# A hybrid decoder trunk with a grouped mixture of experts: ScalarE issues the up matrices' reloads

## The chip, the cores and the metric

The kernel runs on one core of a Trainium2 chip. The metric is the device time of one launch in microseconds (us); the median of several launches is given. The engines of the core are TensorE (PE in the profile; its weight loads are PEld), VectorE (DVE), ScalarE (ACT), GpSimd (POOL) and SyncE (SP). SP does nothing but issue transfers (DMAs); ACT and POOL can issue transfers too. All transfers are carried by the core's 16 DMA engines.

## The reference, cut to what matters

```python
def moe_ffn(x, router_w, router_b, w1, w3, w2):
    e_idx, gates = route(xf, router_w, router_b)      # top group, then 2 of its 8 experts
    ...
    def one_block(args):
        toks, e = args
        xb = x_pad[toks]
        hb = jax.nn.silu(xb @ w1[e]) * (xb @ w3[e])
        return hb @ w2[e]
    ...
def reference(x, ...):
    for l in range(DEPTH):                            # DEPTH = 2
        mix = hybrid_mixer(x, ...)
        x = layer_norm(ALPHA * x + mix, ln1_g[l], ln1_b[l])
        ffn = moe_ffn(x, router_w, router_b, w1[l], w3[l], w2[l])
        x = layer_norm(ALPHA * x + ffn, ln2_g[l], ln2_b[l])
    return x
```

There are 256 tokens of width 1024, two layers, and 64 experts in each. Each expert has a gate matrix `w1` and an up matrix `w3` (1024 x 256) and a down matrix `w2` (256 x 1024), all float32, so each of the three is 1 MB (1.0486 million bytes).

## The kernel before

Both layers do the same: a token mixer (projections, three kinds of attention, an output projection), then routing, then the experts. The experts of a layer are worked through in 16 batches of 4 (`NB = 4`). A batch needs 12 matrices, 12 MB, and every matrix of all 64 experts is read, since the order of the work doesn't depend on which experts are chosen. The texts below number the batches of a layer 0 to 15, and the four experts of a batch k = 0 to 3.

**Buffers.** There are two sets of slots, `w_even` and `w_odd` in the profile: batch j uses the set of its parity. In a set each k has a slot for gate and up matrix side by side (`w13_slots[parity][k]`, gate first) and one for the down matrix (`w2_slots[parity][k]`). Both sets for batches 0 and 1 are loaded (but for one down matrix) before the experts begin. A slot is loaded for batch j + 2 once batch j is through with it.

**TensorE, one batch (`batch`, line 1081).** For k = 0 to 3 it multiplies the gathered tokens by gate and up matrix at once (`up_gate`, line 1030, L1040 in the profile; it waits for `w13_in[parity][k]`, which counts both transfers, and raises `part_psum`). Then it folds the partial sums (L1053) as soon as VectorE has copied those of k = 0 and 2 and ScalarE those of k = 1 and 3. It turns the gates (L1059), gathers the tokens of the next batch (L1025), turns the hidden rows (L1066), multiplies them by the four down matrices (L1072, raises `y2_psum`), and adds the rows to the output (L1078). Then the next batch begins. The last batch of a layer is cut finer: its last gate matrix has a semaphore of its own (`w1_last_in`), and its down matrices come in six pieces (`w2_last_in`, LAST_COLS), filled up with idle multiplications (L609).

**SyncE (`load_first`, line 467; `load_batch`, line 473).** One queue issues everything. For batch j + 2 it waits for `part_psum` of batch j, k; issues gate and up matrix of that k (L380); after the four k it waits for `y2_psum` of batch j and issues the four down matrices (L384). Then it goes on to the next batch, and behind the last batch to the next layer's first weights.

**ScalarE, one batch (line 1828).** It copies the partial sums of k = 1 and of k = 3 (`copy_partial`, L1657), takes a tanh (`squash`, L1822), and makes three more copies: the turned gates, half of the gathered tokens, half of the output rows. Each waits for TensorE. In the first batch of a layer it also seeds the output banks with x (`seed`) between the copies of k = 1 and 3. In the kernel before ScalarE issues one transfer in all, at the very start.

Of the kernel before, what the change touches and what calls it, by code (L numbers as in the profile page):

```python
# [29 lines left out]
NE, NG, EPG, FE, TOP_K = 64, 8, 8, 256, 2  # L30
BLK = 32
NB = P // BLK
BATCHES = NE // NB
# [47 lines left out]
def program(nc, a, consts, const_at, out):  # L81
# [10 lines left out]
    w1 = a["moe_w1"].rearrange("l e (p c) f -> (l e) p (c f)", c=DC)  # L92
    w3 = a["moe_w3"].rearrange("l e (p c) f -> (l e) p (c f)", c=DC)
# [5 lines left out]
    with ctx:  # L99
# [16 lines left out]
        def w13_views(mem):  # L116
            return [mem[:, k * W13:(k + 1) * W13].rearrange("p (m c f) -> p m c f", m=2, c=DC) for k in range(NB)]
# [4 lines left out]
        w13_slots = [w13_views(w13_even), w13_views(w13_mem)]  # L122
# [148 lines left out]
        w13_in = [[Signal(f"w13_{parity}_in{k}") for k in range(NB)] for parity in ("even", "odd")]  # L271
# [55 lines left out]
        def after(eng, l, sig, n):  # L327

            eng.wait_ge(sig.sem, l * sig.per_layer + (n + sig.start))

        def plain(eng):

            eng.sem_inc(passed.sem, 1)
# [5 lines left out]
        def start_batches(eng, base, l):  # L339

            after(eng, l, routed, 1)
            plain(eng)
            m = eng.value_load(iters[0:1, 0:1], min_val=BATCHES - 2, max_val=BATCHES * MAX_ROUNDS - 2)
            return m, batches_before(eng, base)
# [13 lines left out]
        def _(sp):  # L358
# [3 lines left out]
            for l in range(DEPTH):  # L362
# [11 lines left out]
                def load_w_out(h):  # L374
                    sp.dma_start(w_out_half[h], w_out[l, :, :, h * 512:(h + 1) * 512]).then_inc(w_out_in[h].sem, 16)

                def load_w13(e, k, parity, last=False):
                    for m, w in enumerate((w1, w3)):
                        sig = w1_last_in if last and m == 0 and k == NB - 1 else w13_in[parity][k]
                        sp.dma_start(w13_slots[parity][k][:, m, :, :].rearrange("p c f -> p (c f)"),  # L380
                                     w[l * NE + e * NB + k]).then_inc(sig.sem, 16)

                def load_w2(e, k, parity):
                    sp.dma_start(w2_slots[parity][k].rearrange("p c d -> p (c d)"),  # L384
# [44 lines left out]

                after(sp, l, comb, 4)  # L430
                load_w13(0, 0, 0)
                load_w13(0, 1, 0)
                after(sp, l, upT_psum, 2)
                load_ln(sp, l, 0)
                after(sp, l, comb, 8)
                load_w13(0, 2, 0)
                load_w13(0, 3, 0)
                load_w_out(0)
# [26 lines left out]
                m, b0 = start_batches(sp, base, l)  # L465

                def load_first(j, back, e, parity, last=False):
                    for k in range(NB):
                        sp.wait_ge(part_psum.sem, (b0 + j) * NB + (part_psum.start + k + 1 - back))
                        plain(sp)  # L470
                        load_w13(e, k, parity, last)

                def load_batch(j, back, e, parity, last=False):
                    load_first(j, back, e, parity, last)
                    sp.wait_ge(y2_psum.sem, (b0 + j) + (y2_psum.start + 1 - back // NB))
                    plain(sp)


                load_first(2, 2 * NB, 2, 0)
                after(sp, l, x0_ready, 2)  # L480
                after(sp, l, x1_ready, 2)
# [8 lines left out]
                with sp.Fori(4, m, 2) as j_even:  # L490
                    for parity in range(2):
                        j = j_even + parity
# [8 lines left out]
                last = l * NE + (BATCHES - 1) * NB  # L501
# [1147 lines left out]
        def _(act):  # L1649
# [6 lines left out]
            def copy(dst, src):  # L1656
                return fn(dst, src, ACT.Copy)  # L1657
# [4 lines left out]
            for l in range(DEPTH):  # L1662
# [126 lines left out]
                def seed(t):  # L1789
                    for h in range(2):  # L1790
                        after(act, l, y_set, 2 * t + h + 1)
                        after(act, l, (x0_ready, x1_ready)[t], h + 1)
                        copy(Y[t][h][:, :], x[:, t, h * 512:(h + 1) * 512]).then_inc(y_seeded.sem, 1)
# [10 lines left out]
                m, b0 = start_batches(act, base, l)  # L1804

                def copy_gathered(g):
                    act.wait_ge(gathered[1].sem, g + 1)
                    copy(xg[:, 4:8, :], bank[3][:, :].rearrange("p (c s) -> p c s", c=4)).then_inc(xg_act.sem, 1)
# [3 lines left out]
                for c in range(2):  # L1812
                    last = fn(xg[:, 4 + c, :], bank[3][:, c * P:(c + 1) * P], ACT.Identity,
                              scale=g_cols[:, 0, 4 + c:5 + c], bias=g_cols[:, 1, 4 + c:5 + c])
                last.then_inc(first_mid_sb.sem, 1)

                def copy_partial(b, k):
                    act.wait_ge(part_psum.sem, b * NB + (part_psum.start + k + 1))
                    copy(partial[:, k, :], bank[k % 2][:, :]).then_inc(part_act.sem, 1)

                def squash():
                    return fn(eg, bank[0][:, 0:FE], ACT.Tanh, scale=0.5).then_inc(eg_ok.sem, 1)  # L1822

                def copy_scatter(b, source):
                    act.wait_ge(scT_psum.sem, b + 1)
                    copy(scatter, source[:, 0:SEQ]).then_inc(scT_sb.sem, 1)

                def batch(j, first=False):
                    b = b0 + j
                    copy_partial(b, 1)  # L1830
                    if first:
                        seed(0)
                        seed(1)
                        after(act, l, y_seeded, 4)
                    copy_partial(b, 3)
                    act.wait_ge(gu_psum.sem, b + 1)
                    squash()
                    copy_scatter(b, bank[1])
                    copy_gathered(b + 1)
                    act.wait_ge(y2_psum.sem, b + (y2_psum.start + 1))  # L1840
                    copy(y_rows[:, 512:1024], bank[3][:, :]).then_inc(y2_act.sem, 1)

                def last_batch(j):
# [12 lines left out]
                    act.wait_ge(y2_psum.sem, b + (y2_psum.start + 1))  # L1856
                    copy(y_rows[:, end:], bank[0][:, 0:DM - end]).then_inc(y2_act.sem, 1)

                batch(0, first=True)
                with act.Fori(1, m) as j:  # L1860
                    batch(j)
                batch(m)
                last_batch(m + 1)
                act.reg_add(base, base, m + 2)
# [20 lines left out]
```

## Time and profile before

| | us |
|---|---|
| median of 3 launches | 1169.85 (1169.73 to 1171.15) |
| the profiled launch | 1170.28 |
| its span, first to last instruction | 1168.3 |
| TensorE busy | 1050.2 (90%) |
| ScalarE busy | 202.5 (17%) |
| VectorE busy | 368.0 (31%) |
| experts of the first layer, TensorE | about 149 to 581 |
| experts of the second layer, TensorE | about 727 to 1158 |

The profile is one launch. Its page gives busy time by engine, then the span in 40 slices of 29.2 us, then groups of instructions and transfers. Some 2.0 us of the profiled launch lie outside the span.

### The profile page before, as it was taken

The page shows a single profiled execution, that of the slowest core. Times are in us where ns is not written, and L with a number is a line of the kernel's source. Part 1 is how long each engine was busy: PE and PEld are TensorE (multiplying, and loading weights), DVE is VectorE, ACT ScalarE, POOL GpSimd, SP SyncE. Part 2 cuts the span into 40 slices and gives each one's busy share as a digit, 9 for nine tenths or more (in the row PEclk, how much of TensorE's full clock was granted, in tenths as well). Part 3 has the DMA queues.
Part 4 walks back from the last instruction along what each step waited for, and adds up shares of the span by engine and source line. Part 5 has one row for each costly group of instructions (what it writes and reads, how often), then busy time and mean ns, then how long its engine had stood idle before and what let it go on. Part 6 is the DMA issues. An engine that isn't in the chain of part 4 may idle for free.

```text
span 1168.3 us, 16442 instructions
## 1 busy us (share of the span) xinstructions
PE 1050.2 (90%) x6190; PEld 590.4 (51%) x6190; DVE 368.0 (31%) x1009; ACT 202.5 (17%) x473; POOL 32.3 (3%) x46
## 2 busy tenths in 40 slices
PE   9999989989988988888999999989988998888885
PEld 6665754445544444444456657445544444444443
DVE  4875541111122111111268657311122111111113
ACT  1244221111111111111121532211111111101011
POOL 0010010000000000000000101000000000000001
PEclk9999999999999999989999999999999999989898
DMA  9957699999999999999995776999999999999997
GB/s 311 334 226 288 271 376 419 420 420 421 421 420 420 422 420 420 421 420 418 385 331 201 280 297 257 412 421 422 418 421 421 420 420 421 420 420 421 421 419 261
DMA packets 94084, 442.70 MB, mean 379 GB/s; under 512 B 18273, under 2 KB 37857, under 8 KB 45921
## 3 DMA queue, kind: packets, MB, share of 16 engines
q1 hardware_dynamic: 93760, 441.60, 94.1%
q0 software_dynamic: 144, 0.58, 0.1%
q8 instruction: 21, 0.34, 0.1%
q14 instruction: 15, 0.11, 0.0%
q10 hardware_dynamic: 144, 0.07, 0.0%
HBM read 441.16 MB, written 1.05 MB: 379 GB/s over the span
## 4 chain that ended last, share of the span: by engine, by line
PE 57%; SPq 29%; DVE 5%; DMA 5%; issue 3%; ACT 1%; POOL 0%; DVEq 0%; POOLq 0%
SPq L380 19%; PE bank L1025 10%; PE bank L1040 10%; SPq L384 10%; PE bank L674 9%; PE bank L1072 6%; PE bank L1078 5%; DMA w_odd<-in_moe_w 5%; PE bank L800 4%; PE bank L664 2%; PE bank L1053 2%; PE bank L934 1%; ACT moe L1657 1%; PE bank L770 1%; DVE moe L1603 1%
## 5 line engine op out<-in xcount | busy, mean ns | idle before, releaser
L1025 PE MATMUL bank<-moe,x 128*128 128x128 f32 x960 | 233.0, 402 | 0.0
L1025 PEld LDWEIGHTS bank<-moe,x 128*128 128x128 f32 x960 | 230.7, 334 | 0.0
L1657 ACT ACTIVATE moe<-bank 128x512 f32<-128x512 f32 (+2 forms) x194 | 102.1, 535 | 728.2 <-PE bank L1040 347.1
L1078 PE MATMUL bank<-moe 128*128 128x512 f32 (+1 forms) x264 | 119.3, 593 | 25.3 <-DVE moe L1603 24.1
L1040 PE MATMUL bank<-w_even,moe 128*32 128x512 f32 x1024 | 115.9, 600 | 14.5 <-DMA w_even<-in_moe_w 13.0
L1040 PE MATMUL bank<-w_odd,moe 128*32 128x512 f32 x992 | 116.6, 616 | 13.2 <-DMA w_odd<-in_moe_w 13.2
L1576 DVE COPY moe<-bank 128x512 f32<-128x512 f32 x64 | 44.3, 692 | 246.0 <-PE bank L1040 245.8
L1078 PEld LDWEIGHTS bank<-moe 128*128 128x128 f32 x264 | 47.2, 189 | 98.6 <-DVE moe L1603 51.3
L674 PE MATMUL bank<-w_even,w_odd 128*128 128x384 f32 x240 | 81.3, 489 | 0.0
L1040 PEld LDWEIGHTS bank<-w_even,moe 128*32 128x32 f32 x1024 | 31.3, 110 | 94.7 <-issue 70.0
L1040 PEld LDWEIGHTS bank<-w_odd,moe 128*32 128x32 f32 x992 | 30.1, 111 | 94.4 <-issue 76.3
L1072 PE MATMUL bank<-w_even,moe 128*32 128x512 f32 x512 | 58.2, 594 | 13.9 <-DVE moe L1595 13.9
L1072 PE MATMUL bank<-w_odd,moe 128*32 128x512 f32 (+1 forms) x544 | 59.1, 570 | 9.6 <-DVE moe L1595 9.6
L1053 PE MATMUL bank<-moe,constants 128*32 128x512 f32 (+1 forms) x272 | 37.1, 616 | 25.4 <-ACT moe L1657 25.4
L674 PEld LDWEIGHTS bank<-w_even,w_odd 128*128 128x128 f32 x240 | 44.5, 190 | 29.1 <-issue 2.0
L1586 DVE SCALAR_TENSOR_TENSOR moe<-moe,bank 128x256 f32<-128x256 f32 x32 | 13.5, 421 | 138.7 <-ACT moe L1822 138.7
L1603 DVE COPY moe<-bank 128x512 f32<-128x512 f32 x32 | 22.1, 692 | 109.2 <-PE bank L1072 109.2
L1514 DVE COPY moe<-bank 128x512 f32<-128x512 f32 x30 | 20.8, 692 | 86.1 <-PE bank L1025 86.1
L1595 DVE COPY moe<-bank 128x256 f32<-128x256 f32 x32 | 13.6, 424 | 101.5 <-PE bank L1066 101.5
L800 PE MATMUL bank<-w_odd 128*128 128x512 f32 x96 | 44.9, 602 | 0.0
L1657 ACT ACTIVATE w_odd<-bank 128x256 f32<-128x256 f32 (+3 forms) x60 | 27.7, 469 | 84.7 <-PE bank L635 27.4
L1072 PEld LDWEIGHTS bank<-w_even,moe 128*32 128x32 f32 x512 | 18.0, 109 | 42.6 <-issue 42.6
(181 smaller groups left out, 821.9 us busy)
## 6 DMA issues: line engine op xcount, KB each, us to landing
w_even<-in_moe_w SPq DMA_DIRECT2D x192, 1024.0 KB, 26.4
w_odd<-in_moe_w SPq DMA_DIRECT2D x188, 1024.0 KB, 26.4
w_even<-in_w_in SPq DMA_DIRECT2D x24, 768.0 KB, 11.5
w_odd<-in_w_out SPq DMA_DIRECT2D x4, 2048.0 KB, 13.7
w_odd<-in_moe_w SPq DMA_DIRECT2D x8, 512.0 KB, 11.1
w_even<-in_w_in SPq DMA_DIRECT2D x4, 416.0 KB, 6.8
w_even<-in_w_in SPq DMA_DIRECT2D x2, 832.0 KB, 8.4
x<-in_x SPq DMA_DIRECT2D x2, 512.0 KB, 5.5
```

Source lines behind the costliest of these rows:

```text
L380: sp.dma_start(w13_slots[parity][k][:, m, :, :].rearrange("p c f -> p (c f)"), w[l * NE + e * NB + k]).then_inc(sig.sem, 16)
L384: sp.dma_start(w2_slots[parity][k].rearrange("p c d -> p (c d)"), w2[l * NE + e * NB + k]).then_inc(w2_in[parity][k].sem, 16)
L674: last = mm(to[:, 0:GW], rows[:, c, :], weights[:, c, :], start=fresh and c == 0, stop=c == DC // 2 - 1, skip_group_check=True)
L800: last = mm(mix_bank[t][h][:, :], oT[:, c, t * P:(t + 1) * P], w_out_half[h][:, c, :], start=c == 0, stop=c == DC - 1, skip_group_check=True)
L1025: last = mm(bank[2 + c // 4][:, c % 4 * P:(c % 4 + 1) * P], xc[:, t, c, :], chosen[:, t, :], start=t == 0, stop=t == 1)
L1040: last = mm(bank[k % 2][BLK * q:BLK * (q + 1), :], xg[:, c, BLK * k:BLK * (k + 1)], w[:, :, c, :], start=c < 4, stop=c >= 4)
L1053: last = mm(to[BLK * k:BLK * (k + 1), 0:cols.stop - cols.start], const("fold"), partial[:, k, cols], start=True, stop=True)
L1072: last = mm(to[BLK * k:BLK * (k + 1), 0:hi - lo], hT[:, c, BLK * k:BLK * (k + 1)], w2_slots[parity][k][:, c, lo:hi], start=c == 0, stop=c ...
L1078: return mm(Y[t][h][:, lo - 512 * h:hi - 512 * h], scatter[:, t * P:(t + 1) * P], y_rows[:, lo:hi], start=False, stop=True, skip_group_che ...
L1576: nc.vector.tensor_copy(partial[:, k, :], bank[k % 2][:, :]).then_inc(part_dve.sem, 1)
L1603: nc.vector.tensor_copy(y_rows[:, 0:512], bank[2][:, :]).then_inc(y2_dve.sem, 1)
L1657: return fn(dst, src, ACT.Copy)
```

## The change

The up matrices of batches 2 to 15 of each layer, 56 transfers of 1 MB a layer, are no longer issued by SyncE but by ScalarE: those of k = 0 and 1 right behind its copy of the partial sums of k = 1, those of k = 2 and 3 behind its copy of those of k = 3. By then TensorE is through with the slots, since the copies wait for the same `part_psum`. SyncE keeps the gate matrices, each behind its own `part_psum`, and the down matrices. The first two batches' matrices are still loaded by SyncE. ScalarE's loop is now written for two batches at a time, since the slots alternate. Transfers, bytes and the instructions of TensorE and VectorE are the same.

```diff
-                def load_w13(e, k, parity, last=False):
-                    for m, w in enumerate((w1, w3)):
+                def load_w13(e, k, parity, last=False, matrices=(0, 1)):
+                    for m in matrices:
                         sig = w1_last_in if last and m == 0 and k == NB - 1 else w13_in[parity][k]
                         sp.dma_start(w13_slots[parity][k][:, m, :, :].rearrange("p c f -> p (c f)"),
-                                     w[l * NE + e * NB + k]).then_inc(sig.sem, 16)
+                                     (w1, w3)[m][l * NE + e * NB + k]).then_inc(sig.sem, 16)
...
-                        load_w13(e, k, parity, last)
+                        load_w13(e, k, parity, last, (0,))
...
-                def batch(j, first=False):
+                def load_up(e, parity, ks):
+                    for k in ks:
+                        act.dma_start(w13_slots[parity][k][:, 1, :, :].rearrange("p c f -> p (c f)"),
+                                      w3[l * NE + e * NB + k]).then_inc(w13_in[parity][k].sem, 16)
+
+                def batch(j, parity=0, e_next=None, first=False):
                     b = b0 + j
                     copy_partial(b, 1)
+                    if e_next is not None:
+                        load_up(e_next, parity, (0, 1))
                     if first:
                         seed(0)
                         seed(1)
                         after(act, l, y_seeded, 4)
                     copy_partial(b, 3)
+                    if e_next is not None:
+                        load_up(e_next, parity, (2, 3))
...
-                batch(0, first=True)
-                with act.Fori(1, m) as j:
-                    batch(j)
+                batch(0, 0, 2, first=True)
+                batch(1, 1, 3)
+                with act.Fori(2, m, 2) as j_even:
+                    for parity in range(2):
+                        j = j_even + parity
+                        batch(j, parity, (j + 2) & (BATCHES - 1))
                 batch(m)
```

ScalarE in its loop over the batches, before. `moe<-bank 128x512` is a copy of partial sums, `128x256` the tanh (L1822) and the turned gates:

```order
L1657 ACTIVATE moe<-bank 128x512
L1818 REGISTER_ALU
L1657 ACTIVATE moe<-bank 128x512
L1836 REGISTER_ALU
L1822 ACTIVATE moe<-bank 128x256
L1657 ACTIVATE moe<-bank 128x256
```

The same place after, in the even half of the loop; each DMA row is one up matrix:

```order
L1657 ACTIVATE moe<-bank 128x512
L1830 REGISTER_ALU x2
L1830 ISA
L1830 DMA w_even<-in_moe_w 128x2048
L1830 ISA
L1830 DMA w_even<-in_moe_w 128x2048
L1818 REGISTER_ALU
L1657 ACTIVATE moe<-bank 128x512
L1830 ISA
L1830 DMA w_even<-in_moe_w 128x2048
L1830 ISA
L1830 DMA w_even<-in_moe_w 128x2048
```

Two issues now stand between the two copies of partial sums, and two more between the second copy and the tanh.

SyncE at the end of a layer, before: `w_odd` of the last batch, gate and up matrix of each k (x2), and then its down matrices in pieces (L504):

```order
L469 REGISTER_ALU
L380 DMA w_odd<-in_moe_w 128x2048 x2
L475 REGISTER_ALU
L504 DMA w_odd<-in_moe_w 128x4x512 x2
L504 DMA w_odd<-in_moe_w 128x4x256 x4
```

The same place after:

```order
L469 REGISTER_ALU
L380 DMA w_odd<-in_moe_w 128x2048
L475 REGISTER_ALU
L504 DMA w_odd<-in_moe_w 128x4x512 x2
L504 DMA w_odd<-in_moe_w 128x4x256 x4
```

In SyncE's queue a batch is now eight transfers, four gate and four down matrices, in place of twelve; the up matrices of the same batch stand in no order to them.

## Rows read from the trace of the kernel before

**Rows 1.** The page: busy time by engine, and GB/s moved in 40 slices.
```profile
PE 1050.2 (90%) x6190; PEld 590.4 (51%) x6190; DVE 368.0 (31%) x1009; ACT 202.5 (17%) x473; POOL 32.3 (3%) x46
GB/s 311 334 226 288 271 376 419 420 420 421 421 420 420 422 420 420 421 420 418 385 331 201 280 297 257 412 421 422 418 421 421 420 420 421 420 420 421 421 419 261
```

**Rows 2.** Stretch, length, busy PE, PEld, DVE, ACT, POOL, clock, DMA share, GB/s.
```profile
480.00:540.00 60.00, 50.15 (x305) 25.77 (x304) 9.89 (x24) 6.88 (x13) 0.00 (x0) 0.94 1.01 420
```

**Rows 3.** SyncE's queue in order of time: start, length, line, transfers issued.
```profile
151.36 5.97 SPq L380 DMA_DIRECT2D w_even<-in_moe_w  x8
171.09 1.75 SPq L384 DMA_DIRECT2D w_even<-in_moe_w  x4
...
359.79 12.68 SPq L384 DMA_DIRECT2D w_odd<-in_moe_w  x4
...
419.64 12.68 SPq L384 DMA_DIRECT2D w_odd<-in_moe_w  x4
...
519.34 19.77 SPq L380 DMA_DIRECT2D w_odd<-in_moe_w  x8
```

**Rows 4.** TensorE, one batch without a wait for data [idle before <-releaser].
```profile
175.40 7.07 PE L1040 MATMUL bank<-w_odd,moe 128*32 128x512 f32 x64
...
193.17 3.64 PE L1072 MATMUL bank<-w_odd,moe 128*32 128x512 f32 x32 [0.61 <-DVE moe L1595]
197.61 3.70 PE L1078 MATMUL bank<-moe 128*128 128x512 f32 x8 [0.80 <-DVE moe L1603]
201.24 7.07 PE L1040 MATMUL bank<-w_even,moe 128*32 128x512 f32 x64
```

**Rows 5.** TensorE, later in the first layer, up to its end.
```profile
417.12 1.92 PE L1040 MATMUL bank<-w_even,moe 128*32 128x512 f32 x16 [2.79 <-DMA w_even<-in_moe_w]
...
447.06 3.34 PE L1040 MATMUL bank<-w_odd,moe 128*32 128x512 f32 x16 [2.99 <-DMA w_odd<-in_moe_w]
...
521.19 3.64 PE L1072 MATMUL bank<-w_odd,moe 128*32 128x512 f32 x32 [0.61 <-DVE moe L1595]
...
536.83 1.92 PE L1040 MATMUL bank<-w_even,moe 128*32 128x512 f32 x16 [2.21 <-DMA w_even<-in_moe_w]
...
561.85 1.92 PE L1040 MATMUL bank<-w_odd,moe 128*32 128x512 f32 x16 [0.44 <-DMA w_odd<-in_moe_w]
...
578.72 0.64 PE L1072 MATMUL bank<-w_odd,moe 128*32 128x256 f32 x8
579.87 1.13 PE L1078 MATMUL bank<-moe 128*128 128x256 f32 x4 [0.51 <-ACT moe L1657]
```

**Rows 6.** Waits of TensorE: us in total, times, the longest.
```profile
PE bank L1040 <- DMA w_odd<-in_moe_w: 13.2, 9, 3.0
PE bank L1040 <- DMA w_even<-in_moe_w: 13.0, 6, 2.8
```

**Rows 7.** The chain that ended last, in order of time.
```profile
534.31 27.42 DMA w_odd<-in_moe_w
```

**Rows 8.** As rows 2, while the last batch's down matrices land.
```profile
566.00:578.00 12.00, 10.83 (x110) 5.46 (x99) 3.36 (x6) 1.54 (x4) 0.00 (x0) 1.00 1.07 365
```

**Rows 9.** ScalarE in one batch, in order of time.
```profile
179.11 0.60 ACT L1657 ACTIVATE moe<-bank 128x512 f32<-128x512 f32 x1 [7.49 <-PE bank L1040]
182.54 0.60 ACT L1657 ACTIVATE moe<-bank 128x512 f32<-128x512 f32 x1 [2.84 <-PE bank L1040]
184.41 0.38 ACT L1822 ACTIVATE moe<-bank 128x256 f32<-128x256 f32 x1 [1.27 <-PE bank L1053]
...
192.36 0.60 ACT L1657 ACTIVATE moe<-bank 128x512 f32<-128x512 f32 x1 [7.23 <-PE bank L1025]
```

**Rows 10.** DMA queues from 14 to 15 us: packets, MB, share of 16 engines.
```profile
q0 software_dynamic: 66, 0.30, 76.3%
q1 hardware_dynamic: 68, 0.09, 26.0%
```

**Rows 11.** The page's transfers: KB each, median us from issue to landing.
```profile
w_even<-in_moe_w SPq DMA_DIRECT2D x192, 1024.0 KB, 26.4
constants<-in_constants POOLq DMA_DIRECT2D x1, 565.5 KB, 7.0
small<-in_mla_q_norm SPq DMA_DIRECT2D x2, 1.0 KB, 2.6
```

## The prediction, made before the change was run

> **What bounds the kernel now.** I read the page's busy shares first: TensorE 90%, ScalarE 17% [rows 1]. That looks like a kernel bound by TensorE. The GB/s line under it says otherwise for the experts: from the seventh slice on it stands at 420 and stays there until the layer's end, in both layers [rows 1], and a stretch taken out of it has the DMA engines busy 1.01 of the time while TensorE has 50.15 us in 60 [rows 2]. In each layer the experts are a race between two things of nearly the same length. A batch of TensorE without a wait for data takes 201.24 - 175.40 = 25.84 us [rows 4]. A batch of transfers, 12 MB, takes longer: SyncE's down matrices of every second batch begin at 359.79 and 419.64, 59.85 us for 24 transfers [rows 3], so 2.494 us for one and 29.93 us for a batch. (1.0486 MB at 420 GB/s is 2.497.) TensorE starts with two batches already loaded and lives on that stock, losing 4.1 us of it with each batch. It runs out at 417, where the first wait for a DMA stands; from then on there are waits of 2 to 3 us, up to the end of the layer [rows 5], 26.2 us in both layers, 13.1 in each [rows 6].
>
> At the layer's end both sides finish together. The up matrix of batch 15, k = 2 lands at 534.31 + 27.42 = 561.73 [rows 7]. Behind it come two transfers of 2.494 and the last 4 MB in pieces at 365 GB/s [rows 8], 11.5 us: all has landed at 561.7 + 5.0 + 11.5 = 578.2. TensorE begins with its last piece at 578.72 and ends the last additions within a microsecond or two of 579.87 [rows 5]. So the sum of the bytes is one bound, and what TensorE still has to do when a given matrix lands is the other. The change leaves the bytes alone and changes what lands when.
>
> **What ScalarE pays.** It gets 56 issues a layer. An issue took SyncE 1.75 / 4 = 0.44 us (L384 at 171.09) [rows 3], so a pair costs 0.88. Between its two copies ScalarE is free from 179.71 to 182.54, 2.83 us, and between the second copy and the tanh 1.27 us; after the tanh and one short copy it idles for 7.23 us more [rows 9]. Both pairs are covered: 0. If the cover goes (issues that wait for room, below) the second copy is late and TensorE's fold with it. In a layer's first batch the seeds stand in the first gap; that costs 0 to 0.9 us, once, while TensorE still has stock, and I take 0. SyncE saves 56 issues a layer, and nothing follows from that: the engines behind it are full already [rows 2, 3].
>
> **What the reordering costs.** This is the term that counts. Before, one queue serves matrices in the order of use, and a transfer lands 26.4 us after its issue [rows 11], since ten or so stand ahead of it. Now the up matrices stand in a queue of their own with at most four in it. They pass everything that SyncE has issued and what it hasn't come to issue. Each passed transfer lands later by the bytes put ahead of it, and it is gate and down matrices, needed sooner, that are passed. The stock in the slots is then too much up and too little gate and down.
>
> How the two queues share is seen once in this trace. At 14 to 15 us GpSimd's transfer of constants ran beside SyncE's full queue, and the engines took 66 packets of one and 68 of the other [rows 10]; the 565 KB landed in 7.0 us though more had been issued before them [rows 11]. Packets of gate and up matrices are of one size, so I take half the rate each while both have work. The Trainium skill (DMA: Bandwidth & Descriptors, section on queues, rings and completion order) states the same, that each DMA engine goes round the queues packet by packet, and in its rules for kernel authors that spreading transfers over issuers brings no bandwidth. By it the sum is the one below; by service in strict order of issue it would be the second rival's, and the packet row agrees with the rule.
>
> Now count back from the end, in the first layer. Behind the last down matrix of batch 13 SyncE's queue still holds 4 gates of 14, 4 downs of 14, 4 gates of 15 and the 4 MB in pieces: 12 x 2.494 + 11.5 = 41.4 us. To that come u up matrices of batch 15 that haven't landed. They are issued in batch 13, behind k = 1 and k = 3. If TensorE waits for its down matrices in each of these batches, one such wait is 29.9 us behind the other; in between it does the downs (3.64), 0.80 of waiting, the additions (3.70) and two k of 7.07 / 4 = 1.77 [rows 4]: the first pair is asked for 11.7 us after the wait, 18.2 before the next. Off that go 0.7 for the copy and some 2.2 to 2.6 in which even a transfer of 1 KB isn't there [rows 11], leaving 15 us, at half the rate 7.5 us or 3.0 transfers. So u = 1, and the last down matrix of batch 13 lands at 578.2 - 41.4 - 2.5 = 534.3.
>
> From the start of those down products TensorE has a fixed piece of work left. Before, they start at 521.19 and the last two additions end at 579.87 + 0.7 = 580.6; without the waits of 2.21 and 0.44 between [rows 5] that is 56.8 us. After: 534.3 + 56.8 = 591.1, **10.5 us later than 580.6.** What is late next? The last gate of 14 lands by 534.3 + 4 x 2.494 + 2.5 = 547 and is needed at 548; the downs of 14 at 557 against 560; all gates of 15 by 567 against 568 for the first. So the chain behind batch 13 is TensorE's. The bounds: with u = 0 the layer ends 12.9 us later, with u = 4 it is 3.0. TensorE's clock adds something unsure: after some waits of 2 to 3 us sixteen products took 3.34 us and after others 1.92 [rows 5], with a mean granted clock of 0.94 there [rows 2]; 0 to 1.5 us a layer, in the range and not in the sum, since such waits were there before.
>
> The second layer has the same batches and the same 420 GB/s, so the sum is 1170.3 + 2 x 10.5 = 1191.3 for the profiled launch, and 0.4 less against the median: **1191 us, 1.8% slower.**
>
> **Rivals.**
> - *The forecast's size is off* counts as the forecast: 1184 to 1198, for u between 0.3 and 2.5 and a rate of transfers up to 0.5% off.
> - *Issues are held up* (slower still). From about 500 us on SyncE spends 19.77 us on eight issues, 2.47 each [rows 3]: it waits for room. If that room is shared, ScalarE waits too, some 1.2 us for its first issue and up to 5.0 for the second, taking turns with SyncE: 6.2 against the 2.83 it has. That is 3.4 us in each batch from about batch 5 to 13, 31 us, of which TensorE's own waits of 13.1 [rows 6] would have taken a part: 17 a layer, 1204. For it: SyncE's queue is indeed blocked. Against it: ScalarE's own queue never holds more than four.
> - *Order of issue* (slower, little). If the engines serve by age, the ups issued 18 and 15 us before a wait land behind it: u = 4, 1176. The packets of [rows 10] speak against it.
> - *Faster.* Two queues keep the engines better fed. One mechanism: each per cent of rate brings the landing at 534.3, 383 us after the first reload at 151.36 [rows 3], forward by 3.8 us. To make good 10.5 it needs 2.8%, 432 GB/s; at 4% it would end at 1161. For it speaks only that I see no second full queue in this stretch; against it a busy share of 1.01 at 420 [rows 2].
> - *No difference.* The passing evens out, because SyncE's backlog is refilled as fast: TensorE ends when the bytes do, at 578.2 as before. It would need u near 4 and some rate gained. 1170.
>
> **How the numbers follow.** Forecast 64%, issues held up 15%, order of issue 7%, faster 6%, no difference 6%, something unseen 2%, slower. 0.2% (2.3 us) is about what a measurement can tell from no change. Faster 6%, same 6%, slower 88%. The range leaves out the faster and the unchanged case and the worse half of the blocked one: 1176 to 1204.
>
> **What would show it.** The GB/s line still at 420 in the same slices, but falling off while TensorE still works at each layer's end. Up matrices issued by ACT with a time to landing under about 12 us, SyncE's at 26 or more. TensorE's waits for DMAs begin before 417, near 350, and stand largely before L1072 (down matrices), which had none; the last of them ends at about 534, and the first layer's additions end near 591. ScalarE's issues at 0.4 to 0.8 us each, and L1053's wait for ScalarE at 0.8 as now; 4 us or more there would be the held-up issues. I would be wrong if the ups take 20 us or more to land, if the rate moves off 420 by more than a per cent, or if ScalarE's copies slip.

## The result, and the profile after

| | before | after |
|---|---|---|
| median | 1170.5 us (1169.7 to 1172.4, 4 launches) | 1195.4 us (1191.9 to 1199.7, 4 launches) |
| ratio | | 1.0209, 95% interval 1.0194 to 1.0223 |
| profiled launch | 1170.28, span 1168.3 | 1196.83, span 1194.9 |
| first layer's last additions end | 580.6 | 593.9 |
| second layer's | 1157.9 | 1184.4 |

The kernel is 2.1% slower, where 1.8% was forecast. Between the two profiled launches 26.6 us lie in the two expert stages, 13.3 in the first and 13.2 in the second.

The page of the kernel after, its answer to [rows 1] and [rows 11]: busy time, GB/s in 40 slices, the queues (q1 is SyncE's, q10 ScalarE's), and the transfers with their size and median us from issue to landing.

```profile
PE 1058.1 (89%) x6190; PEld 592.9 (50%) x6190; DVE 367.9 (31%) x1009; ACT 202.2 (17%) x473; POOL 32.3 (3%) x46
...
GB/s 314 321 217 287 296 365 420 421 421 420 420 420 421 421 421 420 420 421 417 333 231 176 282 282 286 410 420 420 421 420 420 420 421 420 421 421 420 421 406 106
...
q1 hardware_dynamic: 77632, 324.15, 68.3%
q10 hardware_dynamic: 16272, 117.51, 23.8%
...
w_even<-in_moe_w SPq DMA_DIRECT2D x136, 1024.0 KB, 34.4
w_odd<-in_moe_w SPq DMA_DIRECT2D x132, 1024.0 KB, 34.7
w_even<-in_moe_w ACTq DMA_DIRECT2D x56, 1024.0 KB, 16.0
w_odd<-in_moe_w ACTq DMA_DIRECT2D x56, 1024.0 KB, 15.9
```

The rate in the full slices is 420 as before; 441.7 MB pass as before, now in two queues. What has changed is how long a transfer takes to land: 16 us on ScalarE's queue, 34.5 on SyncE's, where all took 26.4. At the end of the second expert stage the rate falls off (406 and 106 in the last two slices, for 419 and 261): the data are there and TensorE isn't done. The end of the first stage has the same, 333 and 231 for 385 and 331, with the next layer's first weights in it.

TensorE in the first layer, beside [rows 5]; in brackets the idle time before and who ended it.

```profile
355.75 5.08 PE L1072 MATMUL bank<-w_odd,moe 128*32 128x512 f32 x32 [4.55 <-DMA w_odd<-in_moe_w]
...
384.44 3.64 PE L1072 MATMUL bank<-w_even,moe 128*32 128x512 f32 x32 [2.00 <-DMA w_even<-in_moe_w]
...
416.85 5.25 PE L1072 MATMUL bank<-w_odd,moe 128*32 128x512 f32 x32 [6.17 <-DMA w_odd<-in_moe_w]
...
476.70 6.04 PE L1072 MATMUL bank<-w_odd,moe 128*32 128x512 f32 x32 [6.16 <-DMA w_odd<-in_moe_w]
...
535.62 5.59 PE L1072 MATMUL bank<-w_odd,moe 128*32 128x512 f32 x32 [5.19 <-DMA w_odd<-in_moe_w]
...
593.21 1.13 PE L1078 MATMUL bank<-moe 128*128 128x256 f32 x4 [0.50 <-ACT moe L1657]
```

Before, every wait for data stood before L1040 [rows 5, 6]. Now the long ones stand before L1072, the products with the down matrices, for which TensorE's list of waits had none before. The last of them ends at 535.62, in batch 13. In both layers together TensorE waits, as its list of waits has it (us in total, times, the longest):

```profile
PE bank L1072 <- DMA w_odd<-in_moe_w: 45.5, 8, 6.8
PE bank L1053 <- ACT moe L1657: 25.4, 32, 0.8
...
PE bank L1072 <- DVE moe L1595: 16.0, 21, 0.9
PE bank L1072 <- DMA w_even<-in_moe_w: 4.6, 3, 2.0
PE bank L1040 <- DMA w_odd<-in_moe_w: 1.9, 4, 0.5
```

That is 52.0 us for data where it was 26.2 [rows 6], 25.8 more. It is near the loss of 26.6 but isn't the same sum. Where TensorE waits for a down matrix it no longer waits for VectorE's copy there, which in the kernel before had this row:

```profile
PE bank L1072 <- DVE moe L1595: 23.5, 32, 0.9
```

So 7.5 of the 25.8 us are idle time that was there already under another name. TensorE's idle time in the whole span rose by 18.7 us (118.1 to 136.8). The other 7.9 are busy time, 1058.1 for 1050.2 with the same 6190 products: products ran slower. TensorE's wait for ScalarE's copies (L1053) is 0.8 us at the longest. ScalarE in batch 13, to be read beside [rows 9]:

```profile
516.99 0.60 ACT L1657 ACTIVATE moe<-bank 128x512 f32<-128x512 f32 x1 [7.49 <-PE bank L1040]
517.27 0.85 ACTq L1830 DMA_DIRECT2D w_odd<-in_moe_w  x2
520.42 0.60 ACT L1657 ACTIVATE moe<-bank 128x512 f32<-128x512 f32 x1 [2.84 <-PE bank L1040]
520.56 0.88 ACTq L1830 DMA_DIRECT2D w_odd<-in_moe_w  x2
```

A pair of issues takes 0.85 to 0.88 us and the second copy starts as soon as TensorE allows, 2.84 us of idle time before it as in [rows 9]. At that time SyncE's own queue is stuck, four issues in 20 us:

```profile
509.39 19.88 SPq L384 DMA_DIRECT2D w_even<-in_moe_w  x4
```

So a queue of SyncE's that is full doesn't make ScalarE wait. What ScalarE would pay with its own queue full isn't shown, since that never held more than four transfers.

The queues from 525 to 530 us in the kernel after (packets, MB, share of 16 engines), while both have work:

```profile
q10 hardware_dynamic: 144, 1.05, 50.5%
q1 hardware_dynamic: 144, 1.05, 50.5%
```

Half each, packet for packet. From 517.3 to 535.5 us ScalarE's queue moved 3.15 MB, 3.0 of the four ups of batch 15. The chain that ended last holds the consequence (start, length): a down matrix of batch 13, issued at 491.65, lands 43.83 us later.

```profile
491.65 43.83 DMA w_odd<-in_moe_w
535.48 0.14 issue
535.62 5.64 PE bank L1072 x32
```

### The profile page after: what moved, and what is told of

It is laid out like the page before. It is cut to its first block, busy times and chain, and to the rows that moved or that the text cites. A ratio compares the mean times of both kernels' runs of the same rounds, so it can differ in the third digit from the quotient of the medians.

```text
span 1194.9 us, 16572 instructions
## 1 busy us (share of the span) xinstructions
PE 1058.1 (89%) x6190; PEld 592.9 (50%) x6190; DVE 367.9 (31%) x1009; ACT 202.2 (17%) x473; POOL 32.3 (3%) x46
## 4 chain that ended last, share of the span: by engine, by line
PE 54%; SPq 22%; DMA 15%; DVE 5%; issue 2%; ACT 1%; POOL 0%; DVEq 0%; POOLq 0%
DMA w_odd<-in_moe_w 15%; SPq L384 14%; PE bank L1040 9%; PE bank L1025 9%; PE bank L674 8%; SPq L380 8%; PE bank L1072 7%; PE bank L1078 5%; PE bank L800 4%; PE bank L664 2%; PE bank L1053 1%; PE bank L934 1%; PE bank L770 1%; ACT moe L1657 1%; DVE moe L1603 1%
## 5 line engine op out<-in xcount | busy, mean ns | idle before, releaser
L1072 PE MATMUL bank<-w_odd,moe 128*32 128x512 f32 (+1 forms) x544 | 74.1, 691 | 50.2 <-DMA w_odd<-in_moe_w 45.5
L1040 PE MATMUL bank<-w_even,moe 128*32 128x512 f32 x1024 | 113.2, 594 | 1.5 <-DVE moe L1551 1.5
L1040 PE MATMUL bank<-w_odd,moe 128*32 128x512 f32 x992 | 111.4, 595 | 2.1 <-DMA w_odd<-in_moe_w 1.9
L1078 PEld LDWEIGHTS bank<-moe 128*128 128x128 f32 x264 | 47.2, 189 | 99.0 <-DVE moe L1603 51.7
L1072 PE MATMUL bank<-w_even,moe 128*32 128x512 f32 x512 | 61.6, 623 | 15.9 <-DVE moe L1595 11.3
L1040 PEld LDWEIGHTS bank<-w_even,moe 128*32 128x32 f32 x1024 | 31.7, 110 | 79.4 <-issue 73.6
L1040 PEld LDWEIGHTS bank<-w_odd,moe 128*32 128x32 f32 x992 | 29.5, 109 | 81.6 <-issue 68.0
L1072 PEld LDWEIGHTS bank<-w_odd,moe 128*32 128x32 f32 x544 | 20.4, 128 | 92.4 <-issue 85.6
L1053 PE MATMUL bank<-moe,constants 128*32 128x512 f32 (+1 forms) x272 | 34.5, 576 | 25.4 <-ACT moe L1657 25.4
L1072 PEld LDWEIGHTS bank<-w_even,moe 128*32 128x32 f32 x512 | 18.7, 113 | 47.4 <-issue 47.4
## 6 DMA issues: line engine op xcount, KB each, us to landing
w_even<-in_w_in SPq DMA_DIRECT2D x24, 768.0 KB, 11.5
```

What stands on the lines that cost most here:

```text
L1040: last = mm(bank[k % 2][BLK * q:BLK * (q + 1), :], xg[:, c, BLK * k:BLK * (k + 1)], w[:, :, c, :], start=c < 4, stop=c >= 4)
L1053: last = mm(to[BLK * k:BLK * (k + 1), 0:cols.stop - cols.start], const("fold"), partial[:, k, cols], start=True, stop=True)
L1072: last = mm(to[BLK * k:BLK * (k + 1), 0:hi - lo], hT[:, c, BLK * k:BLK * (k + 1)], w2_slots[parity][k][:, c, lo:hi], start=c == 0, stop=c ...
L1078: return mm(Y[t][h][:, lo - 512 * h:hi - 512 * h], scatter[:, t * P:(t + 1) * P], y_rows[:, lo:hi], start=False, stop=True, skip_group_che ...
```

## The experiments

Three theories stood against each other. **A, passing:** the bytes and their rate are the same, but a matrix in the short queue passes gate and down matrices that are needed sooner. **B, the issuer:** ScalarE's issues cost by themselves. **C, two queues:** the DMA engines do worse with two. All runs stand in one table; us, medians of four launches (ten for e5), ratios to launches of the kernel before taken beside each (medians 1170.0 to 1171.3) with their 95% intervals, and the end of the first layer's additions in the profiled launch (before: 580.6).

| run | what | expected (by A, but for e4) | measured | ratio | first layer ends |
|---|---|---|---|---|---|
| e10 | changed kernel again | 1192 to 1197 | 1195.2 | 1.0209 (1.0192 to 1.0226) | 594.3 |
| e5 | ups of batches 2 to 7 by ScalarE | 1170 to 1172 | 1172.4 | 1.0011 (1.0001 to 1.0021) | 581.2 |
| e6 | ups of batches 8 to 15 by ScalarE | 1195 | 1194.2 | 1.0193 (1.0176 to 1.0210) | 594.3 |
| e7 | ups of even batches by ScalarE | 1176 to 1180 | 1183.0 | 1.0102 (1.0085 to 1.0119) | 586.2 |
| e8 | ups of odd batches by ScalarE | 1189 to 1192 | 1190.3 | 1.0165 (1.0148 to 1.0182) | 590.2 |
| e2 | ups of k = 0, 1 by ScalarE | 1176 to 1178 | 1182.3 | 1.0101 (1.0084 to 1.0118) | 584.0 |
| e3 | even batches' downs by ScalarE, no ups | 1189 | 1190.3 | 1.0168 (1.0151 to 1.0185) | 588.8 |
| e1 | ups one batch later | 1176 | 1196.5 | 1.0221 (1.0204 to 1.0238) | 592.7 |
| e9 | as e1, but full queues at the start | 1182 | 1179.1 | 1.0075 (1.0058 to 1.0092) | 583.7 |
| e4 | idle products before odd downs | 1191 | 1235.1 | 1.0549 (1.0531 to 1.0566) | 614.2 |

Five medians are more than 2 us off what was expected: e4 by 44, e1 by 20, e2 by 4, e7 and e9 by 3.

### Early against late: e5 and e6

```diff
 e5, ScalarE:
+                for j in range(1, 6):
+                    batch(j, j % 2, j + 2)
+                with act.Fori(6, m) as j:
+                    batch(j)
 (SyncE: matrices=(0,) for batches 2 to 7, (0, 1) from 8 on; e6 the other way round)
```

> ScalarE issues the ups of batches 2 to 7 only, two batches ahead as in the changed kernel; from batch 8 on SyncE issues gate and up together, as in the kernel before. Theory A (passing): what counts is what stands behind batch 13's down matrices at the end, and there the order is that of the kernel before: each layer ends at 580.6 as before, 1170 to 1172, though 24 of the 56 issues are ScalarE's. Theories B (ScalarE's issues cost by themselves) and C (two queues move data worse): 24/56 of the changed kernel's 25 us, about 1181.

> The counterpart: SyncE issues all up to batch 7, ScalarE the ups of batches 8 to 15. Theory A: the order at the end is the changed kernel's, so the whole loss, 13 us a layer, about 1195, with the last wait before L1072 of batch 13 ending near 535. Theories B and C: 32/56 of 25 us, about 1184.

ScalarE issues 24 matrices a layer in e5 at a price of 0.1%, and 32 in e6 at the full price of the changed kernel with 56. TensorE's last long wait of the first layer is back before L1040 in e5 (L1044 there, 1.88 us where the kernel before has 2.21), and in e6 it stands before the downs of batch 13 (L1076 there), as in the changed kernel. First e5, then e6:

```profile
537.41 1.92 PE L1044 MATMUL bank<-w_even,moe 128*32 128x512 f32 x16 [1.88 <-DMA w_even<-in_moe_w]
```
```profile
533.99 5.92 PE L1076 MATMUL bank<-w_odd,moe 128*32 128x512 f32 x32 [4.51 <-DMA w_odd<-in_moe_w]
```

B and C forecast 1181 and 1184 and are out by 9 and 10 us. The passing of the early batches leaves little: the first layer ends 0.6 us late. Once the short queue is no longer fed, the order is the old one again, and the end is set by what stands behind the last matrices.

### Even against odd: e7 and e8

> ScalarE issues the ups of the even batches 2 to 14, SyncE those of the odd ones: 28 issues a layer. Theory A by the count from the landing of everything at 578.2: behind batch 13's last down matrix stand 4 gates of 14, 4 downs of 14, 8 of 15 and the pieces: 16 x 2.494 + 11.5 = 51.4, it lands at 526.8 where it is needed at 521.2, and the layer ends 3 us late plus 1.5 for the slower products after a wait: 1176 to 1180. Batch 14's last gate lands at 536.8 as before. Theories B and C: half the loss, as e8.

> The other half: ScalarE issues the ups of the odd batches 3 to 15, also 28 a layer. Theory A: behind batch 14's last gate and up stand its 4 downs, 4 gates of 15 and the pieces, 20.0 + 11.5 = 31.5, the ups of 15 have landed: it lands at 546.7 where it was 536.8, and the layer ends at 590.1, 9.5 us late and some more for slower products: 1189 to 1192, with long waits before L1040 of the even batches. So the two halves differ by 10 us or more. Theories B and C: both halves cost the same, about 1183.

The same number of issues, 28 a layer, and 7.3 us between them, where I had expected 10 or more. B and C forecast 1183 for both: e7's 1183.0 alone would suit them, but e8's 1190.3 doesn't, and they have nothing by which the halves could differ. e8 came out as counted, batch 14's last gate and up at 547.1 (forecast 546.7):

```profile
542.21 3.61 PE L1040 MATMUL bank<-w_even,moe 128*32 128x512 f32 x16 [3.13 <-DMA w_even<-in_moe_w]
547.12 1.92 PE L1040 MATMUL bank<-w_even,moe 128*32 128x512 f32 x16 [1.30 <-DMA w_even<-in_moe_w]
```

e7 cost more than counted, 1183.0 for 1176 to 1180, and its waits stand elsewhere than I said, before L1040 of batch 13:

```profile
512.39 3.32 PE L1040 MATMUL bank<-w_odd,moe 128*32 128x512 f32 x16 [2.95 <-DMA w_odd<-in_moe_w]
517.30 1.92 PE L1040 MATMUL bank<-w_odd,moe 128*32 128x512 f32 x16 [1.59 <-DMA w_odd<-in_moe_w]
```

The following count was made after the run. I had counted behind the downs of 13 and the gates of 14 and not behind the last gate and up of 13. Behind it stand 4 + 4 + 4 + 8 transfers and the pieces, 20 x 2.494 + 11.5 = 61.4, so it lands at 516.8, measured 517.3. In the kernel before, the ups of 14 stand behind it too, 24 transfers, and it lands at 506.8; that is when TensorE uses it. The count has to be made for every kind of matrix of the last three batches, and the largest delay is the one that stands.

### Half the ups, and other matrices: e2 and e3

> Half a dose: ScalarE issues only the ups of k = 0 and 1 of each batch, two batches ahead as in the changed kernel; SyncE issues those of k = 2 and 3 with the gates. Theory A by the same count: behind batch 13's last down matrix 12 + 4 transfers of SyncE and the pieces, 51.4 us, the two ups of 15 have landed (15 us at half the rate are 3): it lands at 526.8, the layer ends at 583.6, 3.0 us later than before the change, not half of the changed kernel's 13; about 1176 to 1178. Theory B: half the issues, half the loss, about 1183. Theory C: two queues run in most of the time, most of the loss, 1185 or more.

In the profiled launch the downs of batch 13 start at 525.95 (counted: landing at 526.8) and the first layer ends 3.4 us late (counted: 3.0). The whole launch took 1178.3; the other three took 1182 to 1183, and their waits can't be seen, so the median of 1182.3 can't be told from theory B's 1183. It decides nothing between A and B.

```profile
525.95 5.34 PE L1072 MATMUL bank<-w_odd,moe 128*32 128x512 f32 x32 [3.00 <-DMA w_odd<-in_moe_w]
```

> Another matrix passes: SyncE issues all gates and ups as in the kernel before, and ScalarE issues the down matrices of the even batches 2 to 14, four in a row, behind its last copy of batch j - 2. 28 issues a layer, none of them ahead of a copy that TensorE waits for soon. Theory A: what is passed now is gates and ups. Behind the last gate and up of batch 14 stand 8 of batch 15 and the pieces, 20.0 + 11.5 = 31.5 us (the downs of 14 have landed): it lands at 546.7 where it was 536.8. TensorE's work from there, 536.83 to 580.6 less 0.44, is 43.3: the layer ends at 590.0, 9.4 us late, about 1189, with waits before L1040 of batch 14 of some 10 us and none before L1072. Theory B: half the issues and off the path, 1170 to 1175.

```diff
 e3, ScalarE, behind its copy of the output rows in the even batches:
+                        act.dma_start(w2_slots[parity][k].rearrange("p c d -> p (c d)"),
+                                      w2[l * NE + e * NB + k]).then_inc(w2_in[parity][k].sem, 16)
 (SyncE: no w2 of even batches from 2 on; gates and ups as before)
```

It isn't about up matrices. Here the downs pass, and the waits move to gates and ups of batch 14 (L1036 there), the last of which starts at 545.67 (counted 546.7). The layer ends 8.2 us late, 9.4 counted; the median is 1.3 us above the forecast, and 15 or more from theory B.

```profile
540.77 3.35 PE L1036 MATMUL bank<-w_even,moe 128*32 128x512 f32 x16 [2.92 <-DMA w_even<-in_moe_w]
545.67 1.92 PE L1036 MATMUL bank<-w_even,moe 128*32 128x512 f32 x16 [1.55 <-DMA w_even<-in_moe_w]
```

### Issuing later: e1 and e9

```diff
 e1, ScalarE:
-                batch(0, 0, 2, first=True)
-                batch(1, 1, 3)
+                batch(0, first=True)
+                batch(1, 0, 2)
...
-                        batch(j, parity, (j + 2) & (BATCHES - 1))
-                batch(m)
+                        batch(j, 1 - parity, (j + 1) & (BATCHES - 1))
+                batch(m, 1, BATCHES - 1)
```

> ScalarE issues the same 56 up matrices a layer at the same two places of a batch, but those of batch j + 1 in batch j, where the changed kernel issues those of batch j + 2 (so they are issued one batch, about 30 us, later; the slots have been free since batch j - 1). Theory A (the up matrices pass gate and down matrices that are needed sooner): the passing shrinks. Counted back from the landing of everything at 578.2, batch 13's last down matrix has behind it 12 transfers of SyncE, the last pieces (11.5 us) and all 4 ups of 15: 16 x 2.494 + 11.5 = 51.4, so it lands at 526.8 or before, and the layer ends at 583.6, 3.0 us after the kernel before: about 1176, and ups land some 16 us after their issue, in time for their use 22 us after it. Theory B (what costs is that ScalarE issues at all, by its time or by holding up its copies): the same number of issues at the same places, so no change from 1195. Theory C (two queues move data worse than one): also about 1195.

This missed by 20 us and looked like theory B or C. The profile has the reason, in the DMA share and GB/s (the last two columns) from 157 to 175 us. First the kernel before, then e1:

```profile
157.00:175.00 18.00, 16.14 (x84) 10.83 (x84) 3.53 (x10) 1.97 (x5) 0.00 (x0) 1.00 1.01 422
```
```profile
157.00:175.00 18.00, 16.33 (x87) 10.80 (x84) 3.53 (x10) 1.93 (x4) 0.00 (x0) 1.00 0.65 254
```

With the ups of batch 2 asked for a batch later the DMA engines ran dry at the start of the stage, 18 x (422 - 254) / 422 = 7.2 us of their time. In a stage bound by bytes that comes back at its end: SyncE's queue got rid of its last piece at 576.2 instead of 569.9. e9 undoes this: SyncE issues the ups of batches 2 and 3 as in the kernel before, and ScalarE those of 4 to 15, a batch later than in the changed kernel.

> The late issue of e1 (ups of batch j + 1 in batch j), but SyncE issues the ups of batches 2 and 3, as in the kernel before, so that the queues are as full at the start as there. Theory A explains e1's 12.1 us in the first layer by two terms. One is 6.4 us by which everything lands later, since from 157 to 175 us the transfers ran at 254 GB/s where the kernel before has 422. The other is passing: behind batch 14's down matrices stand 4 gates of 15, the pieces and one up of 15, 24.0 us, so they land at 578.2 - 24.0 = 554.2 where they are needed at 549.7, and TensorE's 30.5 us from there, with 1.5 for slower products, end 5.6 us late. Here the first term should be gone and the second stay: GB/s of 420 from 157 to 175, the last down wait in batch 14, each layer 5 to 6 us late, about 1182. If e1's loss was something else that comes with ScalarE's late issue, it stays at 1194 to 1197.

The same stretch in e9, and then TensorE's last long wait of the first layer:

```profile
157.00:175.00 18.00, 15.59 (x82) 10.64 (x83) 4.00 (x11) 2.52 (x5) 0.00 (x0) 1.00 1.01 422
```
```profile
524.11 6.27 PE L1072 MATMUL bank<-w_odd,moe 128*32 128x512 f32 x32 [4.01 <-DMA w_odd<-in_moe_w]
```

e1 lost 25.7 us against the launches beside it, e9 9.1: 16.6 us are gone with the first transfers' places. Two dry starts of 7.2 us would be 14.4; the rest isn't separated, and ScalarE has eight issues a layer fewer in e9. What is left, 9.1 us, is near the forecast's 12, but not where I put it: the last long wait of the first layer was in batch 13 and not 14, and the layers of the profiled launch (the slowest of the four) lost 3.1 and, by the second layer's end at 1168.6, 7.6 us. Which parity the waits settle on isn't settled by the count. Still, of all kernels in which ScalarE goes on issuing ups to the end this one is the cheapest, with 48 issues a layer: later is better, as A has it.

### The slower products after a wait: e4

```diff
+                    if parity:
+                        keep_warm(32, bank[0])
                     for k in range(NB):
                         pe.wait_ge(w2_in[parity][k].sem, (b0 + j) * 8 + (16 - 16 * l * parity))
```

> The changed kernel, with 32 idle products of 128 columns (some 4 us) put before the down products of the odd batches, where it waits 5 to 6 us for its down matrices. Question: how much of the loss is TensorE's slower products after that wait (32 down products took 5.59 us in batch 13, 3.64 without a wait before them). If the idle time is what lowers the clock, the products take 3.64 again and each layer ends 1.9 us earlier: 1195 - 4 = 1191. If not, 1195. If the idle products cost more than they save in the batches without a wait (1, 3, 5), they only use up stock and the end stays.

The idle products cost far more than they could save; the experiment was ill chosen. I had put them at 4 us; they took 7.38 us in each of seven odd batches a layer (64 product records), 51.7 us a layer. That uses up the stock, the DMA waits vanish altogether, and TensorE alone sets the time. So its question, how much of the loss the slower products make, has no answer from this run. It says one thing: directly behind idle products the 32 down products of the odd batches took 3.64 us each time, and the mean granted clock of the launch is 0.996, where the changed kernel has 5.08 to 6.04 us after its long waits in the first layer and 0.971. It doesn't say that idle time is what decides: in batch 0, after only 0.87 us, the down products took 5.32. Batch 0, and then an odd batch late in the second layer:

```profile
167.85 5.32 PE L1072 MATMUL bank<-w_even,moe 128*32 128x512 f32 x32 [0.87 <-DVE moe L1597]
...
1159.46 7.38 PE L609 MATMUL bank<-constants 128*128 128x128 f32 x64 [0.55 <-DVE moe L1597]
1166.78 3.64 PE L1072 MATMUL bank<-w_odd,moe 128*32 128x512 f32 x32
```

### The changed kernel again: e10

> The changed kernel once more, unaltered, beside e9 and on its chip: 1192 to 1197, with the last wait before L1072 of batch 13 ending within 2 us of 535 in the first layer. It tells how far the waits of single launches differ, for the comparison of e6 (1194) with it.

Down products of batch 13 start at 535.59 (535.62 in the first set of launches) and take 6.00 us; the long waits stand before L1072 of odd batches again.

## Why the prediction was right, and where it was off

**The bound.** Right: the rate stayed at 420 GB/s, and the bytes were not what moved.

**ScalarE's price, taken as 0.** Right. A pair took 0.85 to 0.88 us for 0.88, and no copy was late. e5 puts the price of 24 issues a layer at 1.0 us (0.1 to 2.5 by its interval) in the whole launch.

**The share.** Half each was taken from one microsecond at the kernel's start [rows 10]. It holds: 144 packets against 144. It is also what the Trainium skill says of queues (DMA: Bandwidth & Descriptors, queues, rings and completion order). The Trainium skill's rule that more issuers bring no bandwidth (the same page, rules for kernel authors) agrees with 420 GB/s before and after.

**The count back from the end.** The term that carried the forecast. Batch 13's downs were to land at 534.3 and land at 535.5; the remaining 56.8 us of TensorE's work took 58.3. Term by term, first layer:

| | forecast | measured |
|---|---|---|
| downs of batch 13 start | 534.3 | 535.6 |
| TensorE from there, at full clock | 56.8 | 56.3 |
| slower products behind the wait | 0 (0 to 1.5 kept for the range) | 2.0 (5.64 for 3.64) |
| end | 591.1 | 593.9 |
| loss | 10.5 | 13.3 |

So the mechanism was right and two sizes were small. The larger is the clock: I left the slower products out of the sum, since the kernel before has waits too. But its last long wait of a layer, 2.21 us, was followed by products at full speed (sixteen in 1.92 us [rows 5]), while the new one of 5.2 us isn't: from 535.6 to 541.2 the mean granted clock was 0.64 of full speed, so by estimate some 70% of that time at the lower of its two levels, 1.2 GHz for 2.4. The same products took 6.00 us in e10. The other 1.3 us stay open. In the profiled launch the queues emptied a little later than before, SyncE's last piece issued by 571.5 for 569.9, and part of it may be the first ups, which ScalarE asks for at 153.5 and 156.9 while the engines have room (216 GB/s from 151 to 157 where it was 281, 0.9 us of their time). But in e10 that piece was issued by 570.2 and batch 13's downs were no earlier, so this isn't shown to be the reason.

**When the waits come.** Partly wrong. They begin at 324, near the 350 I gave, and stand before L1072, but not in every batch: in the first layer 4.6 to 6.2 us in the odd ones from 7 to 13, and 2.0 or less in the even. The count assumed one wait each 29.9 us. It survived because all it used was the time from the issue of batch 15's ups (517.3) to the landing (535.5), 18.2 us, and that came out the same; with it came u, the ups still to land: 3.0 of four had passed, so u = 1 as counted. That the 18.2 came out is in part luck. It was worked out from a wait in every batch, while the last two long waits ended 58.9 us apart, with none in batch 12 between them.

**Ups landing in under 12 us.** Wrong: 16 in the median. At half the rate a pair takes 10 us and two pairs stand in each other's way. I had the rate for that and didn't use it. A landing of 20 us was named as a refutation, and single ones reached it (at most 20.4 between 300 and 540 us) without the mechanism failing: the mark was set badly.

**The rivals.** Issues held up: out, by ScalarE's 0.85 us beside SyncE's 20 for four. Order of issue: out, by the packets. Faster and no difference: out.

## What to carry to other kernels

Where the DMA engines are full, as here, a second queue isn't more bandwidth but a second order: it got half the rate while it had work, and what it carried passed everything that waited in the first queue. Ask of each transfer that is moved which ones it will pass and which of them is needed first, and count back from the last byte of the stage to every matrix of the last batches. And when a transfer is issued later on purpose, see first that the queue doesn't run dry: e1 lost 7 us of DMA time in the first 20 us of a stage and paid for it 400 us later.

## What the runs showed of the hardware that I had not expected

- A full SyncE queue didn't hold up ScalarE: with SyncE blocked at 5 us an issue (four in 19.88), ScalarE's DMA instructions took 0.34 us each.
- Two queues with 8 KB packets shared the 16 DMA engines to the packet, 144 and 144 in 5 us, at an unchanged 420 GB/s.
- After waits of 4.6 to 6.8 us, both layers of the changed kernel taken together, the next 32 products of 512 columns took 4.9 to 6.5 us in place of 3.64. After shorter ones it goes either way, and the length of the wait doesn't order it: 3.64 after 2.00 us at 384.44, but 5.34 after 1.50 at 324.27, both in the changed kernel, and 5.31 after 0.89 at 322.19 in e2.
- The launches of the changed kernel spread more than those of the kernel before: 1191.9 to 1199.7 and, in e10, 1193.5 to 1199.1, against 1169.7 to 1172.4 and 1169.7 to 1173.0. It isn't common to all kernels with two queues: e1, e6 and e8, in which they interleave to the end too, spread by 1.5 to 2.9 us, e2 by 4.9. Why wasn't tried.
